# Layer 0's queries computed token by token, in halves of the heads, among the first block's attention

## What is computed

```python
h = modulate(rms_norm(x, norm1_gain[i]), sh1, sc1)
y = h @ w_qkv[i]                    # 8 query heads, 2 key heads, 2 value heads, of 128
q = rms_norm(q, q_gain); k = rms_norm(k, k_gain)       # per head
q = apply_axial_rope(q, cos, sin); k = apply_axial_rope(k, cos, sin)
# layer 0: every token attends to 256 context tokens and all 256 tokens
s = einsum('bqgrd,bkgd->bgrqk', q, ka) * scale
o = einsum('bgrqk,bkgd->bqgrd', softmax(s), va)
x = x + g1 * (o @ w_o[i])
h2 = modulate(rms_norm(x, norm2_gain[i]), sh2, sc2)
# per block of 128 tokens: top 16 keys for each of 8 heads, 128 experts a token, u and v gathered
x = x + g2 * peer_ffn(h2, peer_w_q[i], peer_sub_keys[i], peer_u[i], peer_v[i])
```

## Time and profile before

| | us |
|---|---|
| median of 3 runs | 3314.36 |
| lowest and highest | 3310.12, 3316.52 |
| the profiled execution | 3314.96 |
| span of its profile | 3312.5 |
| TensorE busy | 3091.8 (93%) |
| VectorE busy | 2124.0 (64%) |
| ScalarE busy | 952.6 (29%) |

### The profile page before, as it was taken

One profiled execution on the slowest core, in us unless ns is written; L12 is line 12 of the kernel. 1 busy time (PEld: TensorE's weight loads), 2 busy tenths in 40 slices (PEclk: granted clock), 3 DMA queues, 4 the chain that ended last, 5 costly groups with the idle time before them and its releaser, 6 DMA issues.

```text
span 3312.5 us, 39746 instructions
## 1 busy us (share of the span) xinstructions
PE 3091.8 (93%) x13271; PEld 2201.6 (66%) x13281; DVE 2124.0 (64%) x4271; ACT 952.6 (29%) x2463; POOL 1222.5 (37%) x1129
## 2 busy tenths in 40 slices
PE   8899999999999999999999899987998999987777
PEld 5588888887887888887887755533534755542224
DVE  6677778765556456865555687577565587587554
ACT  2220012221001002221002465334446364443333
POOL 1002545343443442353440044444444044444432
PEclk9999999999999999999999999999999999999999
DMA  8487998788998996688995699999999799999998
GB/s 341 171 285 290 364 372 304 257 327 336 357 352 338 366 345 233 240 324 338 372 353 211 231 417 420 420 419 400 402 422 421 294 418 421 421 421 422 421 422 354
DMA packets 251172, 1160.93 MB, mean 350 GB/s; under 512 B 27160, under 2 KB 34680, under 8 KB 184976
## 3 DMA queue, kind: packets, MB, share of 16 engines
q0 software_dynamic: 152784, 825.30, 61.9%
q1 hardware_dynamic: 98192, 333.71, 27.7%
q10 hardware_dynamic: 48, 0.05, 0.0%
HBM read 1157.85 MB, written 1.10 MB: 350 GB/s over the span
## 4 chain that ended last, share of the span: by engine, by line
PE 64%; DMA 18%; DVE 7%; ACT 5%; issue 2%; POOL 0%; SPq 0%; ACTq 0%; DVEq 0%; POOLq 0%
PE ps_b L1437 18%; PE ps_a L1372 12%; DMA ring<-in_peer_uv,idx 12%; PE ps_a L1445 9%; PE ps_b L753 6%; PE ps_a L740 4%; DMA arena<-in_peer_uv,idx 4%; ACT arena L1663 3%; DVE ring L2780 2%; PE ps_b L1201 2%; PE ps_b L762 1%; ACT L1663 1%; PE ps_b L1142 1%; PE ps_b L1194 1%; DMA ring<-in_ffn 1%
## 5 line engine op out<-in xcount | busy, mean ns | idle before, releaser
L1372 PE MATMUL ps_a<-ring,arena 128*128 128x512 f32 x1728 | 820.3, 609 | 134.8 <-ACT arena L1663 134.2
L715 POOL DMA_INDIRECT ring<-in_peer_uv,idx x448 | 496.9, 1109 | 901.4 <-PE ps_a L1372 629.1
L2780 DVE SCALAR_TENSOR_TENSOR ring<-ring,h_tm 128x1024 f32<-128x1024 f32 x448 | 546.8, 1223 | 379.7 <-DMA ring<-in_peer_uv,idx 379.0
L675 POOL DMA_INDIRECT ring<-in_peer_uv,idx_now x512 | 579.0, 1131 | 423.4 <-DVE arena L2608 160.5
L1372 PEld LDWEIGHTS ps_a<-ring,arena 128*128 128x128 f32 x1728 | 308.8, 191 | 567.7 <-ACT arena L1663 298.4
L1437 PE MATMUL ps_b<-x_t,ring 128*128 128x256 f32 x2816 | 623.6, 380 | 2.1 <-DMA ring<-in_ffn 1.3
L1437 PEld LDWEIGHTS ps_b<-x_t,ring 128*128 128x128 f32 x2816 | 533.7, 190 | 80.7 <-issue 3.5
L1663 ACT ACTIVATE arena<-ps_b 128x256 f32<-128x256 f32 (+3 forms) x214 | 101.8, 476 | 1258.7 <-PE ps_b L1437 829.5
L1445 PE MATMUL ps_a<-arena,ring 128*128 128x256 f32 x1408 | 318.7, 380 | 0.0
L2608 DVE SCALAR_TENSOR_TENSOR arena<-ring,h_tm 128x1024 f32<-128x1024 f32 x256 | 299.5, 1221 | 22.2 <-DMA ring<-in_peer_uv,idx_now 21.8
L1445 PEld LDWEIGHTS ps_a<-arena,ring 128*128 128x128 f32 x1408 | 267.8, 190 | 39.0 <-issue 3.5
(11 more groups left out here) (439 smaller groups left out, 3370.4 us busy)
## 6 DMA issues: line engine op xcount, KB each, us to landing
ring<-in_ffn SPq DMA_DIRECT2D x264, 512.0 KB, 7.0
wring<-in_second_w SPq DMA_DIRECT2D x166, 512.0 KB, 5.4
wring<-in_mix_w SPq DMA_DIRECT2D x128, 512.0 KB, 6.1
ring<-in_ada_rows POOLq DMA_DIRECT2D x36, 512.0 KB, 5.9
ring<-in_second_w SPq DMA_DIRECT2D x12, 1024.0 KB, 9.8
ring<-in_peer_uv,idx_now POOLq DMA_INDIRECT x512, 8.6
ring<-in_peer_uv,idx POOLq DMA_INDIRECT x448, 14.8
arena<-in_second_w SPq DMA_DIRECT2D x13, 512.0 KB, 10.5
```

The source lines that it names most:

```text
L675: G.indirect_dma_start(rows[:, s, :], None, table, bass.IndirectOffsetOnAxis(ap=idx_now[:, half, s:s + 1], axis=0)).then_inc(rows_in[s], p ...
L715: G.indirect_dma_start(pairs[slot].rearrange("p c d -> p (c d)"), None, a["peer_uv"], bass.IndirectOffsetOnAxis(ap=idx[:, b, s:s + 1], axi ...
L1372: ins = mm(ps_a[:, b * D + j * 512:b * D + (j + 1) * 512], diags[:, at % DIAGS, :], pairs[at % PAIRS][:, 1, j * 512:(j + 1) * 512], start= ...
L2780: V.scalar_tensor_tensor(row, row, 1.0, h_tm[:, n // SLOTS, :], ALU.mult, ALU.mult, accum_out=dots[:, n % SLOTS:n % SLOTS + 1]).then_inc(d ...
```

## The change

Layer 0's queries are computed token by token: a 128x128 piece of `h2` (one block's tokens) is stationary and 512 columns of weights, four heads, move. There are four such halves, (block, half of the heads): (0,0), (0,1), (1,0), (1,1). Each uses four chunks, laid out anew and appended to the weights (`FIRST_Q`), and each chunk is used up by four matmul records. The two halves of the heads are loaded once for each block. Per half, ScalarE makes four squares with their sums and a root of 128x4, VectorE scales, rotates and adds in five steps with a table that holds the gain (`rope_x0`, a new load ahead of the first double load, made ready by six small VectorE operations), TensorE turns it by four transposes, and ScalarE copies it to `qk_n`.

The halves (0,0) and (0,1) stand ahead of the attention, (1,0) around scores 0 and 1, (1,1) between half-groups 1 and 2. The turn of (1,1) is inside the output projection. Scores alternate between the two bank pairs; values of all half-groups use one bank of `ps_b`.

```diff
-        HALF_AT = 0, 0, 0, D
+        HALF_AT = 0, D, 0, D
...
-            chunk_loads(a["second_w"], FIRST_ADA, 2 * WR)
+            chunk_loads(a["second_w"], FIRST_ADA, WR)
+            chunk_loads(a["second_w"], FIRST_Q, WR)
...
-            for i in range(0, AHEAD_CHUNKS // 2, 2):
-                query_loads(0, FIRST_ADA, i, i + 2)
-                if i < QKV_CHUNKS - 2 * WR:
-                    chunk_loads(a["second_w"], FIRST_ADA + 2 * WR + i, 2, i)
+            eng.dma_start(rope_x0, a["rope"]).then_inc(rope_in, 16)
+            for i, at in enumerate((WR, 0, WR)):
+                query_loads(0, FIRST_ADA, 2 * i, 2 * i + 2)
+                chunk_loads(a["second_w"], FIRST_Q + at, WR)
             chunk_loads(a["second_w"], FIRST_ADA + QKV_CHUNKS, WR)
...
+            def first_query(b, half, k0, k1):
+                bank = ps_b[:, 512:D] if (b, half) == (0, 1) else ps_b[:, 0:512]
+                for k in range(k0, k1):
+                    if k % 2 == 0:
+                        chunk(k // 2)
+                    ins = mm(bank, h2[:, k, b * P:(b + 1) * P], wring[:, k // 2, k % 2 * 512:(k % 2 + 1) * 512],
+                             start=k == 0, stop=k == KT - 1)
+                    if k % 2:
+                        ins.then_inc(chunk_done, pe.adds(chunk_done))
...
             def block_attention():
+                fm_group(0, ps_b[:, 0:512], h2, mod_ready)
+                mod_row_free()
+                tm_group(2, ps_b[:, 512:D], h2)
+                qk_stats(0, 4, True)
+                first_query(0, 0, 0, KT)
+                eng.wait_ge(qkv_taken, pe.next(qkv_taken))
+                first_query(0, 1, 0, KT)
+                query_turn(0, 0, ps_c[:, :], q_tm0)
+                eng.wait_ge(oq_taken, pe.next(oq_taken))
+                first_query(1, 0, 0, 2)
+                half_scores(0, 0, False)
                 half_scores(0, 1, False)
-                qk_stats(4, 3, True)
+                first_query(1, 0, 2, KT)
+                query_turn(0, 1, ps_d[:, :], q_tm0)
+                eng.wait_ge(pt_taken, pe.next(pt_taken))
                 half_weights(0, probs_c[0])
-                half_values(0, pt_c[0], 1)
                 half_scores(0, 2, False)
+                eng.wait_ge(oq_taken, pe.next(oq_taken))
+                half_values(0, pt_c[0], 512, 1)
                 half_weights(1, probs_c[1])
                 half_scores(0, 3, False)
-                half_values(1, pt_c[1], 0)
+                half_values(1, pt_c[1], 512, 1)
+                query_turn(1, 0, ps_c[:, :], q_tm0)
+                eng.wait_ge(oq_taken, pe.next(oq_taken))
+                first_query(1, 1, 0, KT)
+                eng.wait_ge(pt_taken, pe.next(pt_taken))
                 for h in range(2, 4):
...
+            def square_sums(raw, unread, sums):
                 for i in range(4):
+                    ins = act(unread[:, i, :], raw[:, i * P:(i + 1) * P], ACT.Square, accum_out=sums[:, i:i + 1])
...
+                act(sums, sums, ACT.Sqrt, scale=1.0 / P, bias=eps[:, 1:2]).then_inc(oq_std, ac.adds(oq_std))
...
+                    ve.skip(chunk_done, 2 * WR + 2 * KT)
+                    eng.wait_ge(rope_in, ROPE_LANDED)
+                    rope_tables(rope_tm0, gain_tm0)
+                    qk_norm(4, True, T)
+                    first_query(0, 0)
+                    first_query(0, 1)
+                    for h in range(2):
+                        half_max(l, h, HALF_AT[h])
+                    for h in range(2):
+                        half_over(l, h, probs_c[h])
+                    first_query(1, 0)
+                    for h in range(2, 4):
+                        half_max(l, h, HALF_AT[h])
+                    for h in range(2, 4):
+                        half_over(l, h, probs_c[h % 2])
+                    first_query(1, 1)
```

More of the change, by code:

```diff
@@ L64 @@
 LAYER_1 = FIRST_ADA + SECOND_CHUNKS
+FIRST_Q = LAYER_1 + ADA_CHUNKS + SECOND_CHUNKS
 GR = 8
@@ L1737, in qkv @@
                 for g in range(4):
-                    if g == 3 and attending:
-                        half_exps(l, 0, 0, probs_c[0])
                     qk_take(l, g)
@@ L2231, in _ @@
                 if l == 0:
-                    qkv(l, 2, True)
                     block_attention(l)
@@ L2344, in query_norm, with first_query, query_step @@
             def query_norm(b, half, raw, step):
-                q, scale = q_tm[b][half], q_scale[:, 4 * half:4 * half + 4]
+                query_step(q_tm[b][half], q_turned, rope_tm[b], q_scale[:, 4 * half:4 * half + 4], raw, step)
+            def first_query(b, half):
+                raw = ps_b[:, 512:D] if (b, half) == (0, 1) else ps_b[:, 0:512]
+                for step in range(4):
+                    query_step(q_tm0[b][half], q_turned0, rope_tm0[b], q_scale0[b][:, 4 * half:4 * half + 4], raw, step)
+            def query_step(q, turned, tables, scale, raw, step):
                 eng.wait_ge(dve_step, ve.now(dve_step))
@@ L3382, in laid_out @@
     consts, masks, window, rope = shape_constants()
-    rope = np.stack([rope[:, 0], rope[:, 1], rows(x["q_norm_gain_2"][1]), rope[:, 2], rope[:, 3]], 1).astype(np.float32)
+    gain = [rows(x["q_norm_gain_2"][l]) for l in range(L)]
+    rope = np.stack([rope[:, 0], rope[:, 1], gain[1], rope[:, 2], rope[:, 3], gain[0]], 1).astype(np.float32)
     return dict(rope=rope, consts=consts, masks=masks, window=window, vecs1=np.concatenate(vecs1, 1),
```

112 lines of the change are left out of this document (63 added, 49 removed).

## The result

The changed kernel takes 3323.04 us (median of nine, 3318.82 to 3327.8), the kernel before 3314.51 (median of nine) beside it: ratio 1.0027, 95% interval 1.0019 to 1.0036, so 8.5 us slower. The forecast was 5.8 us more, 3320.3, in a range of 3310 to 3327.

A forecast was written before the change was run, and what follows sets the result against it. The DMA-bound gathers set the pace after a chain holding the changed stage, so its shift reaches the end: 3.5 + 3.0 - 0.65 = +5.9 us, 3320.8 on the profiled execution, given as 3320.3 for the median; range 3310 to 3327.

The forecast's parts named there:

- Where the time goes: Gathers from 1920 on fill the DMA engines; a shift of the changed stage's end moves the kernel's end by as much.
- First wait for loads: Before half (0,1), TensorE waits 3.5 us for its first chunk, queued behind the second double load and the table.
- Second: Before half (1,0), TensorE waits 3.4 us for its first chunk, behind three chunks and two double loads.
- ScalarE's chain: Before the values of half-group 1, ScalarE's and VectorE's serial order lasts until 1847.6; TensorE waits 5.6 us.
- The output projection's start: The output projection begins at 1865.9 instead of 1862.4: +3.5 us.
- The output projection: Inside it, a 2.9 us wait for the fifth chunk, an old 0.3 wait gone, a turn of 0.44 added: +3.0.
- The table load of the norm: Before the next norm, ScalarE's table load of 1.28 us goes; the mean behind it takes half: -0.65 us.
- Table loads on ScalarE: Two switches on the path, taken as 1.28 us each without a drain; the skill's rule would add 2.8 us, giving 3323.1.
- the clock falls: Rival, 12%: a 5.6 us wait on TensorE lowers its clock, 1.6 us each time, once or twice: +2.2, 3322.5.
- the queue is slower: Rival, 22%: chunks next to double loads cost 1.44 us on average rather than 1.25: +4, 3324.3.
- the loads are not late: Rival, 18%: chunks are served beside double loads, so the waits of 3.5 and 3.4 go: -1, 3313.3.
- The bound of -11.9: Rival, 8%: TensorE hardly waits in the stage, 5.1 us less work and 6.8 idle filled by queries: 3302.4.

The follow-up runs named there:

- c_after: The changed kernel itself, unaltered, run again beside the follow-up runs on a slower chip: 1.0028 of the kernel before.
- e3: The changed kernel with products of no use filling three of TensorE's waits: 1.0023 of the kernel before.
- e1: The changed kernel with each half query's four chunks issued ahead of the two double loads instead of behind them: 1.0036 of the kernel before.
- e8: The changed kernel with double loads behind the last query chunk, seven kept loads ahead of the output projection's chunks, ScalarE and VectorE reordered: 0.9985 of the kernel before.
- e11: e8 with SyncE's kept and double loads spread behind the query chunks and among the output projection's chunks: 3301.6 us, 0.9966 of the kernel before.
- e12: e8 with all nine kept loads again behind the output projection's first four chunks: 1.0000 of the kernel before.
- e7: The changed kernel with all six double loads behind the last chunk of half (1,1): 1.0006 of the kernel before.
- e2: The changed kernel with seven of nine kept loads issued ahead of the output projection's chunks: 1.0019 of the kernel before.

## Why the prediction was nearly right

- **Where the time goes.** A shift of the stage is carried through: shown by the table's last column.
- **First wait for loads**, 3.5 forecast: 3.37. The chunk landed 8.35 us after its issue, behind the double loads, as stepped.
- **Second**, 3.4: 1.90, because half (0,1) took 1.77 longer. The chunk itself came when forecast: in the times of the trace of before (3.57 more, by the first mark) at 1823.7 for 1823.6.
- **ScalarE's chain**, values of half-group 1 at 1847.6: there they are at 1847.6. The wait is 4.93 for 5.6 as TensorE's other work ended 0.7 later.
- **The output projection's start**, +3.5: measured from the first mark, 67.21 against 61.75, +5.5. The difference is the group of 3.68 us (+1.78) and 0.2 in small errors.
- **The output projection**, +3.0: 19.66 against 14.95, +4.7. 1.5 of it are the slow group behind the wait. The wait itself, 3.28 for 2.9, is near by luck: in the times of before the fifth chunk landed at 1878.8 and not at 1876.5, as half (1,1) ended 1.7 later and the issues of the kept loads took 1.3 longer than stepped; but TensorE too came for it at 1875.6 and not at 1873.6. Where TensorE came later still, in c_after, the wait was 0.46. (These issues are thirteen and not twelve, before as after; the sum doesn't use their number.)
- **The table load of the norm**, -0.65: the part from the mean products to the gathers is 0.52 shorter, and so in every run.
- **Table loads on ScalarE**: 1.28 us, and the root 0.01 behind. The Trainium skill, "ScalarE: Activation LUTs", section "What ACT_TABLE_LOAD costs", has about 2.66 for a switch. By that it would be an estimated 1.4 more for each of the two; this trace doesn't agree, as the arrival at 1847.6 leaves no room for it.

So the step that was mis-sized is the clock, which the sum has at nothing. The stage and the part behind it are 9.65 us longer; 5.9 were forecast, and the two slow groups on the path (1.78 and 1.49) are 3.3 of the 3.8 left. Two faults of reading are in it. The rival "the clock falls" was priced about right per fall (1.6 for 1.5 to 1.8), but was set as another world with 12%, though its cause, waits of over 3 us, was a part of the forecast itself: it belonged into the sum. And its chance was taken from one row, in which 3.25 us without a matmul were followed by full clock. The second trace of the same kernel shows 0.54 behind the same wait. The Trainium skill, "TensorE: Matmul & The Clock Gate", Part 1, says that the array is throttled by default and activity releases it; e3 agrees, with 7.13 us for 8.80 where fillers ran in the wait.

Of the other rivals, "the queue is slower" came in only where more was queued ahead of a chunk (10.34 and 15.18 us in e1 and e8), and "the loads are not late" not at all. The bound of -11.9 "if queries fill every gap" was no fantasy: e11 reaches -10.8 in the stage. I had given it 8%; it needed the orders of SyncE, ScalarE and VectorE to be rewritten.

Not settled is why the rest of the span varies by 4 us between traces, and so why the medians differ by 8.5 to 9.1 and the stage with the next part by 9.65. Why a wait of 2.94 or 3.25 is followed by a fall in one execution and not in the next stays open too; no run was made for it.

## What to carry to other kernels

When work is interleaved to fill one engine's gaps, list what the fill adds to each other queue, and step the queues through: here the new loads, squares and copies stood ahead of exactly what TensorE wanted next, in three queues. Rewriting those orders turned 8.5 us of loss into 11 of gain with the same work. And price each wait of about 3 us or more on TensorE with the slow products behind it as well, in the sum and not as a case apart; a wait of about 2 us may bring them too. Last, a wait read from one trace is not what its removal gives: where a load is late behind TensorE, as the fifth chunk here, what is won or lost ahead of it partly goes into its wait.

## What was not expected of the hardware

- A fall of the clock cost 1.5 to 1.8 us in the first trace, with the engine at 0.5 to 0.6 of its full clock for some 3.5 us. In other traces it cost up to 3.0, with the groups behind counted (e1, behind 4.93). Some cases: 7.88 for 5.52 behind a wait of 7.38 us (e8), 9.85 for 7.31 behind 9.34 (e12), 10.19 for 7.31 behind 3.57 (e7), and 6.18 instead of 3.61 from one group of values to the next behind 2.94 (c_after).
- Counted over the stage in all fourteen traces, 19 of the 20 waits of 3.0 us and more were followed by slow products (the one of 3.25 in the first trace of before was not), 9 of the 18 waits of 1.7 to 2.94, and none of the shorter ones. The same wait of 2.94 was followed by slow products in 6 traces of 9.
- Seven products of no use, 3.2 us, in a wait of 3.4 kept the clock up though a gap of 1.03 was left.
- The issue of a DMA, mostly 0.4 us on SyncE, took up to 9.46 behind a backlog (e12) and 4.72 in the changed kernel. The kernel before had one of 5.33 at the same kept load, with nothing urgent behind it; in e2, where seven kept loads had gone ahead, that load's first piece took no more than 0.65. Loads that nobody waits for can so hold up the issue of one that is waited for.
- The same program on other chips took 0.4% longer, the changed kernel with a mean granted clock of 0.986 instead of 0.994 in the two profiles (0.988 and 0.991 in the median of all executions), while a difference between two kernels stayed the same (1.0028 for 1.0027).
